# Two-layer decoder trunk on one core: the order of expert rows and front parts on each engine, from slot tables to a plan by dependences

## The chip, the core and the metric

One core of a Trainium2 chip runs the whole program; the other cores are idle. The metric is device time in microseconds (us), lower is better. Everything is float32.

## What is computed

Two layers over 512 tokens of width 1024. Each layer adds a mixer block (four head groups: chunked gating, dilated attention, short convolution, stick-breaking attention, between one input and one output projection) and then a product-key expert block (PEER). The reference, cut to what matters here:

```python
def reference(x, ...):
    for l in range(2):
        h = _rms(x, g_mix_norm[l])
        x = x + _mixer_block(h, w_in[l], ...)       # w_in 1024 x 2816, w_out 1024 x 1024
        h = _rms(x, g_ffn_norm[l])
        x = x + _peer(h, w_peer_q[l], peer_sub_keys[l], peer_u[l], peer_v[l])

def chunk(xc):                                       # 128 tokens of _peer
    q = (xc @ w_q).reshape(C, 8, 2, 128)
    s = einsum('thpd,hpkd->thpk', q, sub_keys)       # 8 heads, 2 halves, 128 keys
    sv, si = top_k(s, 16)
    cand = sv[:, :, 0, :, None] + sv[:, :, 1, None, :]
    top, pos = top_k(cand, 16)                       # 16 of 256 pairs, eidx = their experts
    g = softmax(top)
    a = einsum('thkd,td->thk', u_tab[eidx], xc)
    w = g * gelu(a)
    return einsum('thk,thkd->td', w, v_tab[eidx])
```

Every token picks 8 x 16 = 128 experts, and for each of them one row of u (4 KB) and one of v (4 KB) is read.

## The kernel before, in words

The work is cut into 8 **steps** (step s = layer s // 4, block of 128 tokens s % 4, called c). A step has 128 **expert rows** q = 128 s ... 128 s + 127: row q is one expert for each of 128 tokens, and 16 rows make a head. For each row

- GpSimd gathers 128 x 8 KB (u and v side by side, 1 MB) into one of NR = 10 places of `ring` (line 467). It waits until the indices of that head are there (`idx_ready`) and until the row that had the place ten rows earlier is used up (`v_used` or `vx_used`);
- VectorE forms the dot product with the token (u row, line 1079);
- ScalarE makes the weight and, for most rows, a 128 x 128 diagonal of it (lines 655, 661, 667);
- the v row is added: by TensorE as two 512-wide matmuls into `psY` (line 822), or by VectorE straight into x (line 1090). Here 204 rows go to VectorE, by fixed tables (`VR`, `VB`, `VF`, `BUSY_ROWS`), and 820 to TensorE.

The **front** of a step is all else: norm, input projection in 11 pieces of 1 MB of weights, attention and so on ("mixer": 4 heads of scores, bias, exponential, weighing, transpose, output; then c + 1 blocks of stick-breaking, each logits, softplus, sums, exponent, exp), output projection in 4 pieces, second norm, and per head the "top" part: query piece, key scores, top keys, top pairs, top index, gate. Steps are taken in groups (0), (1), (2, 3), (4, 5), (6, 7), which share a piece of weights. Pieces have two buffers (`wr`, NW = 2): SyncE loads the next one when the piece two before is done. Gathers of a step can only start when its top index is there, so the front of a later group runs beside the rows of an earlier one. A front part at c = 3 has four stick-breaking blocks, at c = 0 one.

What sets the order: every engine is a queue in program order, with semaphore waits inside. `part_tables` gives each front part a slot number: start of its group + rate x its place in a hand-made pattern, other rate in the top part. Each engine then walks through slots q = 0 ... 1023 and does in slot q the u row q (VectorE), the weight of row q - 1 (ScalarE), the v row q - 3 (TensorE, VectorE), and then the front parts of that slot:

```python
for q in range(SLOTS * STEPS + ROW_LAG):
    r = q - ROW_LAG
    by, m = V_NO.get(divmod(r, TOPK), (1, 0))
    if by == 0:
        ...
    for part, s, i in at_slot("pe", q):
        front(s, part, i)
```

Names the text uses: scores line 711, logits 726, sums 775 and 777, stick out 784 (the end of a mixer's chain on TensorE), gating matmul 791, pieces 694 and 698, key scores 803, transposes 680, top index 1050, first of the top keys 863.

Of the kernel before, what the change touches and what calls it, by code (L numbers as in the profile page):

```python
# [10 lines left out]
ACT = mybir.ActivationFunctionType  # L11
AX = mybir.AxisListType

P = 128
# [3 lines left out]
NC = SEQ // P  # L18
STEPS = DEPTH * NC
KD = D // P  # L20
H, HD = 4, 64
# [21 lines left out]
NG = 1  # L43
ROW_LAG = 3
VROW_LAG = 3
# [9 lines left out]
def mixer_parts(s, at):  # L55


    end = 20 + 6 * (s % NC + 1)
    p = [("act", at + t, part, 0) for t, part in
         ((14.5, "v squares"), (19, "conv taken"), (end + 2, "cat squares"), (end + 5, "catT"))]  # L60
    p += [("pe", at + t, part, 0) for t, part in ((18, "conv"), (21, "sgu"), (end, "stick out"), (end + 4, "catT"))]
    p += [("dve", at + t, part, 0) for t, part in
          ((16.5, "sgu in"), (15, "conv"), (19.5, "dil out"), (22, "sgu"), (end + 1, "stick out"), (end + 3, "cat"))]
    for h in range(H):
        o = at + 4 * h
        p += [("pe", o, "scores", h), ("dve", o + 1, "bias", h), ("act", o + 2, "dil exp", h),
              ("dve", o + 3, "weigh", h), ("pe", o + 4, "dil T", h), ("act", o + 5, "dil taken", h),
              ("pe", o + 6, "dil out", h)]
    for i in range(s % NC + 1):
        o = at + 20 + 6 * i  # L70
        p += [("pe", o, "logits", i), ("act", o + 1, "logits", i), ("dve", o + 2, "softplus", i),
              ("pe", o + 3, "sums", i), ("dve", o + 4, "exponent", i), ("act", o + 5, "stick exp", i)]
    return p, at + end


def top_parts(at):

    return [("pe", at, "key scores"), ("act", at + 0.5, "key scores"), ("dve", at + 1, "top keys"),
            ("dve", at + 2, "top pairs"), ("dve", at + 2.75, "top index"), ("act", at + 3.5, "gate exp"),
            ("dve", at + 4.5, "gate")]  # L80


def front_parts(steps):

    p, a, n = [], steps[0], len(steps)

    def add(parts, s):
        p.extend((eng, t, part, s, i) for eng, t, part, i in parts)

    for j, s in enumerate(steps):  # L90
        o = 4 * j
        add([("act", o, "norm1", 0), ("dve", o + 1, "norm1", 0), ("pe", o + 2, "hT1", 0), ("act", o + 3, "hT1", 0)], s)
    start = 4 * n
    for i in range(N_IN):
        o = start + 2 * n * i
        add([("pe", o, "piece", i), ("pe", o + n / 2, "rest of piece", i), ("act", o + 1.25 * n, "piece", i)], a)
    for j, s in enumerate(steps):
        o = start + 8 * n + 6 * j
        add([("act", o, "qk squares", 0), ("dve", o + 1, "qk", 0), ("pe", o + 3, "qk", 0), ("act", o + 4, "qk taken", 0)], s)
    out = 18 if n == 1 else 50  # L100
    for s in steps:
        parts, out = mixer_parts(s, out)
        add(parts, s)
    out += 6
    gap = 1.5 if n == 1 else 2 * n
    for i in range(N_OUT):
        o = out + gap * i
        add([("pe", o, "piece", N_IN + i), ("pe", o + n / 2, "rest of piece", N_IN + i), ("dve", o + 1.25 * n, "out", i)], a)
    second = out + N_OUT * gap - 1
    for j, s in enumerate(steps):  # L110
        o = second + 4 * j
        add([("act", o, "norm2", 0), ("dve", o + 1, "norm2", 0), ("pe", o + 2, "hT2", 0), ("act", o + 3, "hT2", 0)], s)
    top = second + 4 * n
    for h in range(PH):
        o = top + (5 * n - n // 2) * h
        add([("pe", o, "piece", N_IN + N_OUT + h), ("pe", o + n / 2, "rest of piece", N_IN + N_OUT + h),
             ("act", o + 1.25 * n, "queries", h)], a)
        for j, s in enumerate(steps):
            p.extend((eng, t, part, s, h) for eng, t, part in top_parts(o + 1.25 * n + 1 + 4 * j))
    return p, top  # L120


def part_tables():

    tables = {"act": [], "pe": [], "dve": []}
    for steps, start, rate, top_rate in GROUPS:
        parts, top = front_parts(steps)
        for eng, t, part, s, i in parts:
            tables[eng].append((start + rate * min(t, top) + top_rate * max(t - top, 0), part, s, i))
    return {eng: sorted(rows, key=lambda row: row[0]) for eng, rows in tables.items()}  # L130


PARTS = part_tables()
FIRST_SLOT = int(min(row[0] for rows in PARTS.values() for row in rows)) - 1
# [29 lines left out]
def vector_rows(J):  # L164


    return BUSY_ROWS.get(J, VR)
# [49 lines left out]
def trunk(nc, x_in, cst_in, w_in, w_out, w_q, subkeys, w_sgu, b_sgu, conv_w, g_mix, g_head, g_ffn,  # L217
# [3 lines left out]
    with ExitStack() as ctx:  # L221
# [254 lines left out]
        def _(act):  # L476
# [170 lines left out]
            for slot in range(FIRST_SLOT, 0):  # L647
                for part, s, i in at_slot("act", slot):
                    front(s, part, i)
            for q in range(SLOTS * STEPS + 1):  # L650
                if q and q % NG == 0:
                    J, k = divmod(q - NG, TOPK)
                    s, n = divmod(q - NG, SLOTS)
                    act.wait_ge(dotted, q)
                    link(nc.scalar.activation(gl[:, J % 2, k:k + NG], adot[:, J % 2, k:k + NG], ACT.Gelu_apprx_tanh))  # L655
# [4 lines left out]
                    for i in range(NG):  # L660
                        last = nc.scalar.activation(wgt[:, J % 2, k + i:k + i + 1], gate[:, s % NS, n + i:n + i + 1], ACT.Copy,  # L661
                                                    scale=gl[:, J % 2, k + i:k + i + 1])
                    last.then_inc(w_ready, 1)
                    act.wait_ge(w_ready, q // NG)
                    for i in range(NG):
                        if V_NO[J, k + i][0] == 0:
                            nc.scalar.activation(ring[:, (q - NG + i) % NR, 0:P], ident, ACT.Copy,  # L667
                                                 scale=wgt[:, J % 2, k + i:k + i + 1]).then_inc(diag_ready, 1)
                for part, s, i in at_slot("act", q):
                    front(s, part, i)  # L670
# [3 lines left out]
        def _(pe):  # L674
# [133 lines left out]
            for slot in range(FIRST_SLOT, 0):  # L808
                for part, s, i in at_slot("pe", slot):
                    front(s, part, i)  # L810
            for q in range(SLOTS * STEPS + ROW_LAG):
                r = q - ROW_LAG
                by, m = V_NO.get(divmod(r, TOPK), (1, 0))
                if by == 0:
                    s = r // SLOTS
# [9 lines left out]
                for part, s, i in at_slot("pe", q):  # L825
                    front(s, part, i)
# [3 lines left out]
        def _(dve):  # L830
# [3 lines left out]
            def link(ins):  # L834

                after(mark(ins))
# [47 lines left out]
            def front(s, part, i):  # L884
# [79 lines left out]
                elif part == "stick out":  # L964
                    dve.wait_ge(sb_out, s + 1)
                    v.tensor_copy(cat[:, 3], psO[:, :MW]).then_inc(pso_free, 1)
# [10 lines left out]
                elif part == "sgu":  # L977
                    dve.wait_ge(sgu_out, s + 1)
                    for h in range(H):
# [91 lines left out]
            for slot in range(FIRST_SLOT, 0):  # L1071
                for part, s, i in at_slot("dve", slot):
                    front(s, part, i)
            for q in range(SLOTS * STEPS + VROW_LAG + 1):
                if q < SLOTS * STEPS:
# [5 lines left out]
                r = q - VROW_LAG  # L1081
                J, k = divmod(r, TOPK)
                by, m = V_NO.get((J, k), (0, 0))
                if by:
                    xs = x[:, r // SLOTS % NC]
                    landed(dve, r)
                    dve.wait_ge(w_ready, r // NG + 1)
# [4 lines left out]
                if r >= SLOTS and r % SLOTS == 0:  # L1092
                    add_peer(r // SLOTS - 1)
                for part, s, i in at_slot("dve", q):
                    front(s, part, i)
# [40 lines left out]
```

## Time and profile before

| | us |
|---|---|
| median of 3 runs | 3071.74 (3071.59 to 3072.9) |
| the profiled execution, its own time | 3072.46 |
| its span in the trace | 3070.7 |
| TensorE busy | 2516.7 (82%) |
| VectorE busy | 2223.3 (72%) |
| ScalarE busy | 1470.0 (48%) |
| bytes moved by DMA | 1210.01 MB, of it 1073.81 MB gathers |
| mean granted TensorE clock | 0.911 |

The span is the time from the first to the last instruction; the execution's own time is 1.8 us more. Busy shares are means over stages that differ, so the text reads them stage by stage. GB/s in a stretch is what all DMA queues of the core moved in it.

### The profile page before, as it was taken

What the parts mean: (1) busy time and instruction counts of PE and PEld (TensorE: products, weight loads), DVE (VectorE), ACT (ScalarE), POOL (GpSimd) and SP (SyncE); (2) the same over time, 40 slices, a digit from 0 to 9 for tenths busy, and PEclk for the clock granted to TensorE, in tenths of its full rate; (3) what the DMA queues carried; (4) which work ended last, traced back from release to release, by engine and by line L of the source; (5) the groups of instructions that cost most, each with busy time, mean ns of one, the idle gap of its engine ahead of it and who ended that gap; (6) DMA issues with size and microseconds to landing.
All of it is one profiled execution on the core that took longest, in us unless ns stands there. A gap on an engine that the chain in (4) does not pass through costs nothing. (4 is left out here: it accounts for less than half of the span.)

```text
span 3070.7 us, 28272 instructions
## 1 busy us (share of the span) xinstructions
PE 2516.7 (82%) x7856; PEld 1431.3 (47%) x7856; DVE 2223.3 (72%) x5194; ACT 1470.0 (48%) x3968; POOL 1220.3 (40%) x1028
## 2 busy tenths in 40 slices
PE   7679778897687898997788998998889898866676
PEld 6546355563354553663354454663436444422222
DVE  2485868668769888557867888658776888866665
ACT  2154625437644555335644555437673555533333
POOL 0133434334334444434443444434444444444443
PEclk8789899998787999998998999998889999988989
DMA  6499999998789999999999999999999999999998
GB/s 277 165 403 412 421 394 421 368 407 340 295 335 409 412 397 401 421 421 421 417 421 421 417 416 412 418 420 415 378 383 410 421 421 422 413 422 422 422 422 350
DMA packets 168923, 1210.01 MB, mean 394 GB/s; under 512 B 20032, under 2 KB 20288, under 8 KB 22336
## 3 DMA queue, kind: packets, MB, share of 16 engines
q0 software_dynamic: 147456, 1073.81, 85.3%
q1 hardware_dynamic: 21312, 134.40, 10.8%
q8 instruction: 65, 1.06, 0.1%
q14 instruction: 90, 0.74, 0.1%
HBM read 1206.03 MB, written 2.10 MB: 393 GB/s over the span
## 5 line engine op out<-in xcount | busy, mean ns | idle before, releaser
L467 POOL DMA_INDIRECT ring<-in_uv,idx x1024 | 1220.1, 1192 | 1827.3 <-PE psY L822 1115.0
L822 PE MATMUL psY<-ring 128*128 128x512 f32 x3280 | 1641.6, 646 | 246.3 <-ACT ring L667 214.4
L1079 DVE CUSTOM_DVE_ANT_0 ring<-ring,htok 128x1024 f32<-128x1024 f32 x1024 | 1232.9, 1221 | 403.6 <-DMA ring<-in_uv,idx 397.0
L822 PEld LDWEIGHTS psY<-ring 128*128 128x128 f32 x3280 | 653.5, 207 | 1031.0 <-issue 1021.0
L655 ACT ACTIVATE gl<-adot 128x1 f32<-128x1 f32 x1024 | 204.1, 199 | 968.7 <-DVE adot L1079 963.8
L667 ACT ACTIVATE ring<-cst,wgt 128x128 f32<-128x128 f32 x820 | 329.3, 402 | 27.4
L694 PE MATMUL psP<-hT,wr 128*128 128x256 f32 (+1 forms) x1664 | 320.3, 349 | 1.6 <-ACT hT L504 1.0
L698 PE MATMUL psP<-wr,hT 128*128 128x256 f32 x1344 | 307.3, 383 | 16.7 <-DMA wr<-in_w_out 11.2
L661 ACT ACTIVATE wgt<-gate,gl 128x1 f32<-128x1 f32 x1024 | 301.7, 295 | 34.1
L694 PEld LDWEIGHTS psP<-hT,wr 128*128 128x128 f32 x1664 | 282.1, 198 | 71.8 <-issue 41.5
L698 PEld LDWEIGHTS psP<-wr,hT 128*128 128x128 f32 x1344 | 258.0, 193 | 86.2 <-issue 30.5
L1090 DVE SCALAR_TENSOR_TENSOR x<-ring,wgt,x 128x1024 f32<-128x1024 f32 x204 | 261.3, 1281 | 21.8 <-issue 21.8
L655 ACT ACT_TABLE_LOAD x129 | 165.5, 1283 | 2.3
L863 DVE MAX8 sv<-later 128x8 f32<-128x128 f32 x128 | 31.1, 284 | 89.9 <-ACT later L635 89.9
L775 PE MATMUL psO<-probs,cst 128*128 128x512 f32 x40 | 33.6, 934 | 71.4 <-DVE probs L945 48.5
L803 PE MATMUL psS<-probs,qdsT 128*128 128x128 f32 x256 | 44.5, 301 | 55.2 <-issue 55.2
L1079 DVE DVE_READ_ACCUMULATOR2_ANT adot<- 128x1 f32 x1024 | 84.0, 82 | 0.0
L643 ACT ACTIVATE nmax_top<-tops 128x1 f32<-128x1 f32 x64 | 12.9, 202 | 145.9 <-DVE idx L1050 145.9
L803 PEld LDWEIGHTS psS<-probs,qdsT 128*128 128x128 f32 x256 | 40.3, 207 | 89.5 <-issue 89.5
L644 ACT ACT_TABLE_LOAD x62 | 79.5, 1283 | 1.1
L680 PE MATMUL psT<-cst,hn 128*128 128x128 f32 x192 | 33.2, 330 | 54.6 <-DVE hn L1004 35.1
L1010 DVE TENSOR_TENSOR x<-x,psP 128x512 f32<-128x512 f32 (+1 forms) x20 | 11.6, 580 | 88.8 <-PE psP L698 88.8
(124 smaller groups left out, 1688.0 us busy)
## 6 DMA issues: line engine op xcount, KB each, us to landing
wr<-in_w_in SPq DMA_DIRECT2D x44, 1024.0 KB, 9.2
wr<-in_w_q SPq DMA_DIRECT2D x40, 1024.0 KB, 9.1
ring<-in_uv,idx POOLq DMA_INDIRECT x1024, 14.3
wr<-in_w_out SPq DMA_DIRECT2D x16, 1024.0 KB, 9.1
ring<-in_w_in SPq DMA_DIRECT2D x11, 1024.0 KB, 17.0
probs<-in_subkeys SPq DMA_DIRECT2D x5, 1024.0 KB, 14.4
ring<-in_w_out SPq DMA_DIRECT2D x4, 1024.0 KB, 20.2
cat<-in_g_ffn SPq DMA_DIRECT2D x5, 512.0 KB, 9.9
```

The costliest lines, as they stand in the source:

```text
L467: pool.indirect_dma_start(out=ring[:, q % NR], out_offset=None, in_=tables[s // NC], in_offset=bass.IndirectOffsetOnAxis(ap=idx[:, s % NS, ...
L644: nc.scalar.activation(gate[:, s % NS, i * TOPK:(i + 1) * TOPK], top, ACT.Exp, bias=nmax_top[:], accum_out=gsum[:]).then_inc(top_exp, 1)
L655: link(nc.scalar.activation(gl[:, J % 2, k:k + NG], adot[:, J % 2, k:k + NG], ACT.Gelu_apprx_tanh))
L661: last = nc.scalar.activation(wgt[:, J % 2, k + i:k + i + 1], gate[:, s % NS, n + i:n + i + 1], ACT.Copy, scale=gl[:, J % 2, k + i:k + i + 1])
L667: nc.scalar.activation(ring[:, (q - NG + i) % NR, 0:P], ident, ACT.Copy, scale=wgt[:, J % 2, k + i:k + i + 1]).then_inc(diag_ready, 1)
L694: last = nc.tensor.matmul(bank[:, half * n * P:(half + 1) * n * P], w[:, k, half * P:(half + 1) * P], hT[:, k, :n * P], start=(k == 0), st ...
L698: last = nc.tensor.matmul(bank[:, half * PW:(half + 1) * PW], hT[:, k, half * P:(half + 1) * P], w[:, k], start=(k == 0), stop=(k == KD - 1))
L775: last = nc.tensor.matmul(psO[:], cst[:, C_TRI:C_TRI + P], soft[:, u % 2], start=True, stop=(i == 0))
L803: last = nc.tensor.matmul(psS[:, b * P:(b + 1) * P], qT[:, QUERY_NO[a, i] % 2, b, j * P:(j + 1) * P], sub[:, 2 * i + b], start=True, stop= ...
L822: last = nc.tensor.matmul(psY[:, b * 512:(b + 1) * 512], ring[:, r % NR, 0:P], ring[:, r % NR, D + b * 512:D + (b + 1) * 512], start=first ...
L1079: v.tensor_tensor_reduce(out=u, in0=u, in1=htok[:, q // SLOTS % NS], scale=1.0, scalar=0.0, op0=ALU.mult, op1=ALU.add, accum_out=adot[:, J ...
L1090: v.scalar_tensor_tensor(out=xs, in0=ring[:, r % NR, D:], scalar=wgt[:, J % 2, k:k + 1], in1=xs, op0=ALU.mult, op1=ALU.add).then_inc(vx_us ...
```

## The change

The slot tables, the lags and the tables of VectorE rows are gone. A planner (`plan_orders`) plays the program through on the host with a cost for each part, dependences (`needs`), counts of shared buffers and a model of loads and gathers, and writes down in which order each engine begins its rows and parts. An engine that is free takes, of what can begin, the item with the earliest due time. A front part is due by the old pattern (`front_times`, other starts and rates), a u row at its landing - 2 us, the weight of a row at the end of its u row + 3.5, a v row at its landing + 6. A v row goes to VectorE only where three or more wait for TensorE, none for VectorE, and the next u row has not landed: 61 rows in all, 963 to TensorE. Instructions, bytes, buffers and gathers are as before, apart from three things: 143 more rows are TensorE's (186 go to it, 43 to VectorE), each with a diagonal made on ScalarE, and VectorE has a wait for `cat_squared` ahead of "sgu" and "stick out".

```diff
-NG = 1
-ROW_LAG = 3
-VROW_LAG = 3
-GROUPS = [((0,), -72, 1.00, 1.00), ((1,), 22, 1.00, 1.10), ((2, 3), 129, 0.70, 1.30), ((4, 5), 339, 1.15, 1.30), ((6, 7), 597, 0.97, 1.55)]
+GROUPS = [((0,), -72, 1.00, 1.00), ((1,), -22, 0.85, 0.95), ((2, 3), 120, 0.85, 1.35), ((4, 5), 355, 1.50, 1.45), ((6, 7), 606, 1.10, 1.40)]
+SLOT_US = 2.65
+U_SLACK = -2.0
+R_SLACK = 3.5
+V_SLACK = 6.0
+PE_ROWS = 3
+MARGIN = 0.2
...
+def plan_orders():
...
+            due[eng, part, s, i] = 150 + SLOT_US * (start + rate * min(t, top) + top_rate * max(t - top, 0))
...
+    def choices(eng):
+        c = []
+        for (e, part), keys in classes.items():
...
+            key = keys[0]
+            if missing[key] or ready[key] > now + 1e-9:
+                continue
+            if (eng, part) in HELD and not left[HELD[eng, part]]:
+                continue
...
+            c.append((due[key], key))
+        if eng == "dve":
+            if state["u"] < SLOTS * STEPS and state["u"] in landed:
+                c.append((landed[state["u"]] + U_SLACK, ("u", state["u"])))
...
+        if eng in rows and rows[eng]:
+            q = rows[eng][0]
+            if ("r", q) in done and (eng == "dve" or q // SLOTS <= state["x"]):
+                c.append((landed[q] + V_SLACK, ("v", q)))
+        return c
+
+    def begin(eng, key):
...
+        elif key[0] == "r":
+            state["r"] += 1
+            by[key[1]] = int(len(rows["pe"]) >= PE_ROWS and len(rows["dve"]) == 0 and state["u"] not in landed)
+            rows["dve" if by[key[1]] else "pe"].append(key[1])
...
+                if c:
+                    begin(eng, min(c)[1])
...
+ORDERS, ROW_BY = plan_orders()
...
-VR = (3, 7, 11, 15)
-VB = (1, 3, 5, 7, 9, 11, 13, 15)
-VF = ()
-BUSY_ROWS = {J: VB for J in range(9, 16)}
-BUSY_ROWS.update({J: VF for lo, hi in ((6, 8), (16, 21), (31, 37), (47, 54)) for J in range(lo, hi)})
...
-            for q in range(SLOTS * STEPS + ROW_LAG):
-                r = q - ROW_LAG
-                by, m = V_NO.get(divmod(r, TOPK), (1, 0))
-                if by == 0:
-                    s = r // SLOTS
+            for name, *where in ORDERS["pe"]:
+                if name == "v":
+                    r = where[0]
+                    m, s = V_NO[divmod(r, TOPK)][1], r // SLOTS
...
-                for part, s, i in at_slot("pe", q):
+                else:
+                    part, s, i = where
                     front(s, part, i)
...
                 elif part == "stick out":
                     dve.wait_ge(sb_out, s + 1)
+                    if s:
+                        dve.wait_ge(cat_squared, s)
```

**First place: TensorE, the first stick-breaking blocks of step 3.** `psS<-qdsT,ksT` is the logits of a block, `psO<-probs,cst` and `psO<-later,cst` its sums, `psO<-tms,sgw` the gating, and `psY<-ring x2` one expert row. Before:

```order
L726 MATMUL psS<-qdsT,ksT 128x128 x4
L822 MATMUL psY<-ring 128x512 x2
L791 MATMUL psO<-tms,sgw 128x64 x4
L775 MATMUL psO<-probs,cst 128x512
L822 MATMUL psY<-ring 128x512 x2
L726 MATMUL psS<-qdsT,ksT 128x128 x4
L822 MATMUL psY<-ring 128x512 x2
L775 MATMUL psO<-probs,cst 128x512
L777 MATMUL psO<-later,cst 128x512
L822 MATMUL psY<-ring 128x512 x4
```

The same place in the change:

```order
L1025 MATMUL psS<-qdsT,ksT 128x128 x4
L1117 MATMUL psY<-ring 128x512 x2
L1090 MATMUL psO<-tms,sgw 128x64 x4
L1117 MATMUL psY<-ring 128x512 x4
L1025 MATMUL psS<-qdsT,ksT 128x128 x4
L1074 MATMUL psO<-probs,cst 128x512
L1117 MATMUL psY<-ring 128x512 x4
L1025 MATMUL psS<-qdsT,ksT 128x128 x4
L1074 MATMUL psO<-probs,cst 128x512
L1076 MATMUL psO<-later,cst 128x512
L1117 MATMUL psY<-ring 128x512 x12
L1025 MATMUL psS<-qdsT,ksT 128x128 x4
```

The logits of the next block now stand ahead of the sums of this one, and all rows between are TensorE's. Counted over the whole order, from the first scores to stick out of a step (in row numbers q, on TensorE): step 1 takes 32 rows before and 15 in the change, step 2 takes 26 and 31, step 3 takes 32 and 40, step 4 takes 29 and 18, step 5 takes 38 and 30, step 6 takes 36 and 37, step 7 takes 44 and 49. Steps 2 and 3 together take 58 and 71, of which VectorE has 29 and 8.

**Second place: TensorE, the top part of step 1.** `psP<-hT,wr x16` is a query piece, `psS<-probs,qdsT x2` the key scores of a head. Before, from the query piece of head 2:

```order
L694 MATMUL psP<-hT,wr 128x128 x16
L822 MATMUL psY<-ring 128x512 x4
L803 MATMUL psS<-probs,qdsT 128x128 x2
L822 MATMUL psY<-ring 128x512 x6
L694 MATMUL psP<-hT,wr 128x128 x8
L822 MATMUL psY<-ring 128x512 x2
L694 MATMUL psP<-hT,wr 128x128 x8
L822 MATMUL psY<-ring 128x512 x2
L803 MATMUL psS<-probs,qdsT 128x128 x2
```

In the change, from the query piece of head 4:

```order
L993 MATMUL psP<-hT,wr 128x128 x16
L1117 MATMUL psY<-ring 128x512 x2
L1102 MATMUL psS<-probs,qdsT 128x128 x2
L1117 MATMUL psY<-ring 128x512 x2
L993 MATMUL psP<-hT,wr 128x128 x16
L1102 MATMUL psS<-probs,qdsT 128x128 x2
L993 MATMUL psP<-hT,wr 128x128 x16
L1102 MATMUL psS<-probs,qdsT 128x128 x2
L993 MATMUL psP<-hT,wr 128x128 x16
L979 MATMUL psT<-cst,hn 128x128 x8
L1102 MATMUL psS<-probs,qdsT 128x128 x2
L1117 MATMUL psY<-ring 128x512 x20
```

Before, every piece has rows within and behind it; in the change the last heads' pieces follow each other and ten rows come in one run behind them. On VectorE it is the same place: between the u rows 100 and 101 stand top pairs and top index of head 3 and the whole top parts of heads 4 to 7, where before three to four u rows stand in each head's.

## Rows read from the trace of the kernel before

**Rows 1.** The page: span, bytes moved.

```profile
span 3070.7 us, 28272 instructions
...
DMA packets 168923, 1210.01 MB, mean 394 GB/s; under 512 B 20032, under 2 KB 20288, under 8 KB 22336
```

**Rows 2.** Windows: us, busy PE, PEld, DVE, ACT, POOL (x count), clock, DMA share, GB/s.

```profile
0.00:128.00 128.00, 88.16 (x436) 75.11 (x436) 37.18 (x136) 29.16 (x61) 0.20 (x4) 0.84 0.50 193
...
150.00:500.00 350.00, 284.02 (x1064) 173.01 (x1064) 260.81 (x656) 172.56 (x463) 128.82 (x109) 0.89 1.00 409
...
550.00:700.00 150.00, 137.91 (x515) 96.99 (x516) 94.82 (x180) 59.15 (x168) 47.19 (x42) 0.93 0.95 379
700.00:900.00 200.00, 136.65 (x409) 72.93 (x408) 153.84 (x283) 134.04 (x263) 68.84 (x57) 0.80 0.83 314
900.00:1250.00 350.00, 298.82 (x904) 170.78 (x903) 297.71 (x830) 172.48 (x496) 151.12 (x124) 0.93 1.00 407
...
1400.00:1650.00 250.00, 198.26 (x569) 105.12 (x569) 187.56 (x366) 135.47 (x351) 109.57 (x92) 0.90 1.01 420
...
2165.00:2350.00 185.00, 160.91 (x508) 89.67 (x507) 131.14 (x239) 112.42 (x262) 76.73 (x66) 0.90 0.95 382
...
2700.00:3050.00 350.00, 232.47 (x418) 87.76 (x416) 214.60 (x316) 114.05 (x393) 163.39 (x139) 0.87 1.01 422
```

**Rows 3.** Waits of all engines in 700:900: us in total, times, longest.

```profile
POOL ring L467 <- DVE x L1090: 77.6, 23, 10.1
POOL ring L467 <- PE psY L822: 47.8, 14, 8.0
...
PE psO L775 <- DVE probs L945: 25.4, 5, 6.5
```

**Rows 4.** TensorE's timeline, steps 2 and 3: start, us, line (first scores, stick out).

```profile
678.63 0.91 PE L711 MATMUL psS<-kdT,qdsT 64*128 64x384 f32 x2
...
757.99 2.89 PE L784 MATMUL psO<-vs,tmq 128*128 128x64 f32 x24
760.81 1.12 PE L711 MATMUL psS<-kdT,qdsT 64*128 64x512 f32 x2
...
870.08 3.79 PE L784 MATMUL psO<-vs,tmq 128*128 128x64 f32 x32 [0.36 <-ACT tmq L600]
```

**Rows 5.** TensorE's timeline: step 0's scores and stick out; scores of steps 4, 5; step 7.

```profile
44.86 0.48 PE L711 MATMUL psS<-kdT,qdsT 64*128 64x128 f32 x2
...
78.16 1.97 PE L784 MATMUL psO<-vs,tmq 128*128 128x64 f32 x8 [2.63 <-ACT tmq L600]
...
1379.86 0.48 PE L711 MATMUL psS<-kdT,qdsT 64*128 64x128 f32 x2
...
1455.27 0.70 PE L711 MATMUL psS<-kdT,qdsT 64*128 64x256 f32 x2
...
2167.90 1.12 PE L711 MATMUL psS<-kdT,qdsT 64*128 64x512 f32 x2
...
2286.01 3.68 PE L784 MATMUL psO<-vs,tmq 128*128 128x64 f32 x32
```

**Rows 6.** TensorE's timeline: a piece that waited, three rows, half a piece of two steps.

```profile
410.96 5.73 PE L698 MATMUL psP<-wr,hT 128*128 128x256 f32 x16 [10.72 <-DMA wr<-in_w_out]
416.53 5.31 PE L822 MATMUL psY<-ring 128*128 128x512 f32 x12
...
894.50 3.62 PE L698 MATMUL psP<-wr,hT 128*128 128x256 f32 x16
```

**Rows 7.** The page's group of the u rows.

```profile
L1079 DVE CUSTOM_DVE_ANT_0 ring<-ring,htok 128x1024 f32<-128x1024 f32 x1024 | 1232.9, 1221 | 403.6 <-DMA ring<-in_uv,idx 397.0
```

**Rows 8.** VectorE's timeline: top keys' first, top index of step 0, head 0.

```profile
121.50 0.49 DVE L863 MAX8 sv<-later 128x8 f32<-128x128 f32 x2 [10.09 <-ACT later L635]
...
129.13 0.17 DVE L1050 SCALAR_TENSOR_TENSOR idx<-pick 128x16 int32<-128x16 f32 x1
```

**Rows 9.** Tile ring on POOL: a gather's time from issue to landing.

```profile
DMA to landing us min/median/max: 5.5/14.3/22.9
```

More of the change, by code:

```diff
@@ L76, in top_parts, with front_times @@
[L76 to L83, printed above, removed]
+SLOT_US = 2.65
[4 more added lines that the diff above has]
+MARGIN = 0.2
+def front_times(steps):
     p, a, n = [], steps[0], len(steps)
-    def add(parts, s):
-        p.extend((eng, t, part, s, i) for eng, t, part, i in parts)
@@ L120, in front_parts @@
     return p, top
-def part_tables():
-    tables = {"act": [], "pe": [], "dve": []}
-    for steps, start, rate, top_rate in GROUPS:
[L127 to L134, printed above, removed]
@@ L137, in at_slot, with cost @@
-def at_slot(eng, slot):
-    return [row[1:] for row in PARTS[eng] if slot <= row[0] < slot + 1]
+def cost(eng, part, s, i):
+    n, w = len(GROUP_OF[s]), s % NC + 1
+    if part in ("piece", "rest of piece"):
+        if eng == "act":
+            return 0.3 * n
+        whole = CB <= i < N_IN or i >= N_IN + N_OUT
+        return 3.5 * n / 2 if whole or n == 2 else 3.5 if part == "piece" else 0.0
+    return {"pe": {"hT1": 1.1, "qk": 1.1, "catT": 1.1, "hT2": 1.1, "scores": 0.25 * w, "dil T": 0.15 * w, "dil out": 0.15 * w,
+                   "conv": 0.3, "sgu": 0.5, "logits": 1.2, "sums": 0.9 if i == 0 else 1.75, "stick out": 0.5 * w,
+                   "key scores": 0.5},
+            "act": {"norm1": 1.2, "norm2": 1.2, "hT1": 2.4, "catT": 2.4, "hT2": 1.1, "qk squares": 1.1, "qk taken": 1.3,
+                    "v squares": 0.4, "dil exp": 0.3 + 0.1 * w, "dil taken": 0.2 + 0.1 * w, "logits": 2.4, "stick exp": 0.7,
+                    "conv taken": 0.4, "cat squares": 1.1, "queries": 0.6, "key scores": 0.4, "gate exp": 0.6},
+            "dve": {"norm1": 2.9, "qk": 5.0, "bias": 0.3 + 0.3 * w, "weigh": 0.2 + 0.15 * w, "dil out": 0.6, "softplus": 1.3,
+                    "exponent": 1.2, "stick out": 0.4, "sgu in": 3.2, "sgu": 0.7, "conv": 2.6, "cat": 4.6, "out": 0.35 * n,
+                    "norm2": 3.6, "top keys": 3.0, "top pairs": 2.8, "top index": 2.9, "gate": 0.2}}[eng][part]
@@ L142, in numbers @@
+ORDERS, ROW_BY = plan_orders()
 def numbers(eng, *names):
-    rows = [row[1:] for row in PARTS[eng] if row[1] in names]
+    rows = [key[1:] for key in ORDERS[eng] if key[0] == eng and key[1] in names]
     return {row: n for n, row in enumerate(rows)}
@@ L1070, in _ @@
             dve.wait_ge(s_cst, 16)
[L1071 to L1075, printed above, removed]
+            for name, *where in ORDERS["dve"]:
+                if name == "u":
+                    q = where[0]
                     J, k = divmod(q, TOPK)
@@ L1091, in _ @@
                                            op0=ALU.mult, op1=ALU.add).then_inc(vx_used, 1)
[L1092 to L1094 removed]
+                elif where[0] == "x":
+                    add_peer(where[1])
+                else:
+                    part, s, i = where
                     front(s, part, i)
```

399 lines of the change are left out of this document (335 added, 64 removed).

## The prediction, made before the changed kernel was run

> **What bounds the kernel now.** Read in this order: the bytes, the windows by stage, the waits where a stage is slow, then the timeline there. The core moves 1210 MB in a span of 3070.7 us [rows 1]. In the last long stretch, 2700 to 3050, nothing but rows is left and the queues move 422 GB/s, the most of any stretch, while TensorE is busy 232 of 350 us [rows 2]. So 422 GB/s is what this mix of transfers gets, and 1210 MB at that rate is 2867 us. The other 203 us are stretches in which the queues were not full. The loss of a stretch is its length x (1 - GB/s / 422), from [rows 2]:
>
> - 0 to 128, before the first gather: 69
> - 150 to 500, rows of step 0 beside the front of step 1: 11
> - 550 to 700, input projection of steps 2 and 3: 15
> - 700 to 900, their mixers: 51
> - 900 to 1250, their top parts: 12
> - 1400 to 1650, mixers of steps 4 and 5: 1
> - 2165 to 2350, mainly the mixer of step 7: 18
>
> The rest (26) is the first gathers, the end, and small change. An order of instructions moves no bytes; it can only win or lose in this list, and outside of the first 128 us and the end some 120 us are to be had at most.
>
> Why 700 to 900 is slow: GpSimd waits there for ring places, 77.6 us for VectorE's v rows and 47.8 for TensorE's [rows 3], while TensorE is busy only 137 of 200 us and VectorE 154 [rows 2]. No engine is full; rows stand in program order behind front parts that wait for each other, as the sums for softplus, 25.4 us [rows 3]. The mixer of step 2 takes from 678.6 to 760.9 (82 us) and that of step 3 from 760.8 to 873.9 (113 us) [rows 4]. Its chain of parts sets this, not the rows: a row needs 1 MB / 422 GB/s = 2.49 us, and the 26 and 32 rows in it need 65 and 80. The excess, 17 + 33 = 50, is the measured loss of 51. That agreement is what I build on: **a mixer costs the queues what its chain needs beyond the rows laid into it.**
>
> **The change, term by term** (against the profiled execution, 3072.46 us).
>
> Mixers of steps 2 and 3. They now have 31 and 40 rows, 77 and 100 us of transfers. With the old chains of 82 and 113 the loss is 5 + 13 = 18 instead of 50: **-32**. The logits of the next block now run ahead of the sums of this one, so that VectorE's and ScalarE's work on them lies beside the sums; a block of step 3 cost about 15 us of its 113. Steps 2 and 3 have seven blocks; I take a little over 1 us from each: **-8**; at most the remaining 18, at least 0.
>
> Mixer of step 7. 2167.9 to 2289.7 is 122 us [rows 5], for 44 rows, 110 us. The order gives it 49 rows, 122 us; step 6 keeps its 36 to 37. Of the 18 lost, **-13**.
>
> Mixers of steps 4 and 5. They lose nothing now: step 4 takes 75.4 us [rows 5] for 29 rows (72). The change gives them 18 and 30 rows, 45 and 75 us. What their chains need is not shown, since transfers pace them. Bounds for step 4: step 0's mixer, the same c with no rows in it, took 44.9 to 80.1, 35 us [rows 5], and above 75. I take 50, and for step 5 no more than its 75: **+6**. Ends 0 and +48 (30 in step 4, 18 in step 5, whose mixer takes 93 of its 95 us from transfers). Step 1, squeezed from 32 rows to 15, has seven weight pieces among them, so 55 us of transfers; its chain is longer than step 0's 35 us by one block of some 15, and has rows in it: I give it +5, and take back 3 for the piece of w_out that TensorE waited 10.7 us for [rows 6], whose rows now stand otherwise: **+2**, ends -8 and +25.
>
> Top part of step 1. VectorE does the tops of heads 3 to 7 with no u row between. One head is 121.5 to 129.3, 7.8 us [rows 8]; a u row is 1.22 + 0.08 [rows 7]. From u row 90 to 110 that is 8 x 7.8 + 20 x 1.3 = 88 us, against 20 gathers and 10 weight pieces at 2.49, 75 us. The excess of 13 is partly covered by what is queued: a gather lands 14.3 us after its issue where 5.5 is the least [rows 9], so some 9 us of transfers are in store. **+6**, ends 0 and +20 (weight pieces that queue behind gathers, as the 10.7 us).
>
> Projection of steps 2 and 3. Half a piece is 3.62 us, a row on TensorE 5.31 / 3 = 1.77 (a row is four records) [rows 6]. Before, rows 130 to 160: 11 x 7.2 + 18 x 1.77 + transposes 2 = 113 us against 41 transfers, 102; an excess of 11, with 15 lost. In the change, rows 112 to 138 with 13 of them VectorE's: 79 + 13 x 1.77 + 2 = 104 against 92. The same within 2: **-2**, ends -10 and +10.
>
> More rows on TensorE. 143 x 1.77 = 253 us of work, and VectorE loses as many rows of 1.3. In 2700 to 3050 TensorE has 118 us idle [rows 2] for 32 of them (57 us). The other 111 (197 us) go where 380 of 2550 us are idle, most of it in mixers. I cost them at **0**; the cover is gone if that idle time is waiting that stays, which is the slow rival below.
>
> Before the first gather. In step 0 "sgu in" now stands before the weighing of head 0 and "conv" before that of head 2; by the old durations head 3 leaves VectorE some 3 us later, and half a query piece stands ahead of the first key scores: **+4**, ends -4 and +8. The end: the last row goes over diagonal and TensorE, **+1**. The two new waits on `cat_squared` ask for work of the step before and cost 0. Top parts of the later groups have the same work: 0.
>
> Sum: -32 - 8 - 13 + 6 + 2 + 6 - 2 + 0 + 4 + 1 = -36. 3072.5 - 36 = 3036, and as the median is 0.7 below the profiled execution, **3036** holds for it too.
>
> TensorE's clock belongs here. In 700 to 900 it was granted 0.80 on average, so some 40% of that time ran at 1.2 instead of 2.4 GHz, with 63 of 200 us idle; in 900 to 1250, with 51 of 350 idle, it was 0.93 [rows 2]. The sum takes each duration as the trace has it and counts nothing for the clock. The Trainium skill (TensorE: Matmul & The Clock Gate, HAM oscillation) says that gaps in TensorE's work put it to half clock and an unbroken supply keeps it at full; the two windows agree. By that rule alone the rows moved to TensorE would partly pay for themselves and the time would come out below the sum, as in the first rival.
>
> **Rivals.**
>
> *Faster: rows flow in all mixers.* If blocks overlap and TensorE, fuller, is rarely at half clock, the losses of 700 to 900, 2165 to 2350 and 550 to 700 go: -51 - 18 - 15 = -84, and the start and the block cost 8: 2996. For it: no engine is full there. Against: chains through three engines remain, and 10 ring places.
>
> *No difference.* A mixer's chain stretches with what is laid into it: 113 us for step 3 with 32 rows, 122 for step 7 with 44 [rows 4, 5]. If it does so at 13 us for 8 rows, and the squeezed steps 1, 4 and 5 lose 20, the gain is gone: 3072. This is also the case in which the plan's costs are so far from the chip's that its order waits as the old one did.
>
> *Slower: TensorE becomes the bound.* Place: the mixers and the pieces beside them. If its idle time in 700 to 900 (63 us) stays and 21 rows come to it (37 us) beside 137 of work, the stage takes 237 instead of the 160 forecast, +77. In the mixers of 4 and 5, 52 us idle and 13 rows more: +23; in 6 and 7 the like, +30. It decides once more than about a quarter of that idle time is left (130 / 4 = 33, the gain). With half of it left: 3036 + 65 = 3101. For it: 186 rows leave VectorE in all, and rows at half clock cost twice. Against: planned orders put rows where old ones put waits, and VectorE gets free.
>
> **How the numbers follow.** Forecast (3010 to 3060) 0.52, rows flow 0.17, no difference 0.12, TensorE the bound 0.19. A difference under 0.2% (6 us) is what a measurement of this kernel can't tell from none. Faster gets the first two and a little of the third, 0.71; same 0.10; slower 0.19. The likeliest case's own range is 3010 to 3060. The range for 8 in 10 goes from 2988, just under the fast rival, to 3098, which leaves out the worse half of the slow one.
>
> **What would show it.** Right: 700 to 900 (step 2's and 3's mixers) at 380 GB/s or more instead of 314; GpSimd's waits for VectorE's rows nearly gone and its waits for TensorE's larger; the granted clock above 0.911; step 3's mixer in 100 to 115 us; a dip of GB/s near 400 to 500 where step 1's top parts stand together; first gather at 130 to 138 us instead of 129.6. Wrong: TensorE near 100% busy in the mixers with queues under 400 GB/s (the slow rival), mixers of steps 4 and 5 under 390 GB/s (their chains need more than I took), or a first gather much later.

## The result, and the profile after

The changed kernel takes 3031.11 us (median of 4 runs, 3028.67 to 3033.62) beside 3071.66 us before (3067.65 to 3072.9): ratio 0.9874, 95% interval 0.9861 to 0.9886. It is 40.6 us faster; the forecast was 36. Every median here and below leaves out the executions in the chip's slow state, of which there were two (E1 once, 3777.73 us; the kernel before once, 6970.06 us). The page of its profile:

```profile
span 3029.1 us, 29251 instructions
...
PE 2654.6 (88%) x8428; PEld 1473.6 (49%) x8428; DVE 2062.3 (68%) x5051; ACT 1513.4 (50%) x4098; POOL 1163.1 (38%) x1028
...
DMA packets 168926, 1210.08 MB, mean 399 GB/s; under 512 B 20032, under 2 KB 20288, under 8 KB 22336
...
L1117 PE MATMUL psY<-ring 128*128 128x512 f32 x3852 | 1815.5, 615 | 274.1 <-ACT ring L965 269.4
```

The bytes are those of [rows 1]. The granted clock is 0.961 on average (0.911 before). So the 41.6 us between the spans must lie in stretches where the queues are not full. Windows of the changed kernel, with columns as in [rows 2]:

```profile
0.00:128.00 128.00, 92.26 (x476) 79.42 (x477) 39.72 (x148) 31.15 (x66) 0.20 (x4) 0.84 0.50 195
150.00:400.00 250.00, 223.56 (x801) 128.39 (x800) 170.14 (x428) 132.55 (x352) 89.81 (x81) 0.98 1.01 421
...
450.00:550.00 100.00, 77.59 (x342) 55.41 (x343) 80.26 (x244) 39.00 (x124) 23.22 (x19) 0.86 0.72 291
550.00:633.00 83.00, 80.60 (x337) 62.23 (x337) 57.17 (x114) 25.88 (x79) 28.14 (x25) 1.00 1.00 400
633.00:821.00 188.00, 169.00 (x518) 83.15 (x517) 131.79 (x248) 150.97 (x313) 85.06 (x71) 0.94 0.97 394
821.00:1150.00 329.00, 298.86 (x925) 171.10 (x925) 278.85 (x798) 165.55 (x474) 136.37 (x120) 0.97 1.01 421
1150.00:1200.00 50.00, 34.89 (x102) 18.98 (x101) 31.82 (x65) 22.42 (x74) 17.87 (x15) 0.82 0.91 365
...
1400.00:1500.00 100.00, 94.41 (x280) 47.68 (x279) 71.03 (x144) 76.86 (x183) 44.99 (x39) 0.95 1.00 410
...
1900.00:2050.00 150.00, 140.54 (x510) 92.48 (x509) 105.81 (x214) 74.19 (x185) 52.28 (x46) 0.95 1.00 410
2050.00:2212.00 162.00, 150.78 (x449) 73.64 (x448) 100.30 (x185) 130.29 (x280) 74.61 (x64) 0.97 0.99 395
```

By the loss formula of the prediction, stretch by stage (us of queue time lost):

| stage | before | after | difference | forecast |
|---|---|---|---|---|
| before the first gather | 69.5 | 68.9 | -0.6 | +4 |
| rows of step 0, front of step 1 up to its last tops | 10.8 | 0.7 | -10.1 | +2 |
| last tops of step 1 (before 500:550, after 450:550) | 0.1 | 31.0 | +30.9 | +6 |
| projection and mixers of steps 2, 3 (550:900; 550:821) | 66.5 | 16.8 | -49.7 | -42 |
| their top parts, up to 1150 (before 1250) | 12.4 | 0.8 | -11.6 | 0 |
| projection of step 4, first part (1150:1200) | in the row above | 6.8 | +6.8 | not seen |
| mixers of steps 4, 5 | 1.2 | 2.8 | +1.6 | +6 |
| 1500 (before 1650) to 2350, with the mixers of 6, 7 | 23.6 | 16.6 | -7.0 | -13 |
| all other stretches (first gathers, last rows, end) | 19.3 | 18.1 | -1.2 | +1 |
| sum | 203.4 | 162.5 | -40.9 | -36 |

The sum is 0.7 us from the 41.6 between the spans, as the rates are whole numbers. The total is near, but three stages are far off: one lost 25 us more than forecast, and two came out 12 us better each. What stands behind GpSimd now, for the whole run (us in total, times, longest):

```profile
POOL ring L769 <- PE psY L1117: 1597.5, 773, 38.5
POOL ring L769 <- DVE idx L1350: 157.0, 6, 129.0
...
POOL ring L769 <- DVE x L1388: 2.0, 1, 2.0
```

Before, VectorE's rows held it for 426.9 us and TensorE's for 1115.0. A wait with full queues costs nothing (ten places are always in use); the one of 38.5 us does. TensorE's timeline of steps 2 and 3, to be laid beside [rows 4]:

```profile
633.63 0.91 PE L1010 MATMUL psS<-kdT,qdsT 64*128 64x384 f32 x2
...
714.99 1.12 PE L1010 MATMUL psS<-kdT,qdsT 64*128 64x512 f32 x2
...
817.71 3.68 PE L1083 MATMUL psO<-vs,tmq 128*128 128x64 f32 x32
```

Both mixers take 633.6 to 821.4, 188 us with 71 rows, where 195 us had 58.

### The profile page after: what moved, and what is told of

Read it like the earlier page. It is cut to its first block and busy times, and to the rows that moved or that the text cites. A ratio compares the mean times of both kernels' runs of the same rounds, so it can differ in the third digit from the quotient of the medians.

```text
span 3029.1 us, 29251 instructions
## 1 busy us (share of the span) xinstructions
PE 2654.6 (88%) x8428; PEld 1473.6 (49%) x8428; DVE 2062.3 (68%) x5051; ACT 1513.4 (50%) x4098; POOL 1163.1 (38%) x1028
## 3 DMA queue, kind: packets, MB, share of 16 engines
q1 hardware_dynamic: 21312, 134.40, 10.9%
## 5 line engine op out<-in xcount | busy, mean ns | idle before, releaser
L1117 PE MATMUL psY<-ring 128*128 128x512 f32 x3852 | 1815.5, 615 | 274.1 <-ACT ring L965 269.4
L769 POOL DMA_INDIRECT ring<-in_uv,idx x1024 | 1162.9, 1136 | 1838.0 <-PE psY L1117 1597.5
L1117 PEld LDWEIGHTS psY<-ring 128*128 128x128 f32 x3852 | 723.0, 195 | 1221.1 <-issue 1214.0
L965 ACT ACTIVATE ring<-cst,wgt 128x128 f32<-128x128 f32 x963 | 386.7, 402 | 31.4
L993 PEld LDWEIGHTS psP<-hT,wr 128*128 128x128 f32 x1664 | 275.3, 195 | 51.0 <-issue 19.1
L1388 DVE SCALAR_TENSOR_TENSOR x<-ring,wgt,x 128x1024 f32<-128x1024 f32 x61 | 78.3, 1283 | 34.2 <-issue 34.2
L997 PE MATMUL psP<-ring,hT 128*128 128x256 f32 x192 | 46.7, 408 | 2.9 <-ACT hT L810 2.9
L1347 DVE TENSOR_TENSOR fm<-pos,cst 128x512 f32<-128x512 uint32 x64 | 44.3, 692 | 2.2
L1348 DVE TENSOR_TENSOR fm<-fm,si 128x512 f32<-128x512 f32 x64 | 44.3, 692 | 2.2
L1349 DVE TENSOR_REDUCE pick<-fm 128x32 f32<-128x512 f32 x64 | 43.9, 686 | 2.2
```

What stands on the lines that cost most here:

```text
L769: pool.indirect_dma_start(out=ring[:, q % NR], out_offset=None, in_=tables[s // NC], in_offset=bass.IndirectOffsetOnAxis(ap=idx[:, s % NS, ...
L965: nc.scalar.activation(ring[:, q % NR, 0:P], ident, ACT.Copy, scale=wgt[:, J % 2, one_col]).then_inc(diag_ready, 1)
L993: last = nc.tensor.matmul(bank[:, half * n * P:(half + 1) * n * P], w[:, k, half * P:(half + 1) * P], hT[:, k, :n * P], start=(k == 0), st ...
L997: last = nc.tensor.matmul(bank[:, half * PW:(half + 1) * PW], hT[:, k, half * P:(half + 1) * P], w[:, k], start=(k == 0), stop=(k == KD - 1))
L1117: last = nc.tensor.matmul(psY[:, b * 512:(b + 1) * 512], ring[:, r % NR, 0:P], ring[:, r % NR, D + b * 512:D + (b + 1) * 512], start=first ...
L1347: link(v.tensor_tensor(hot, pos[:, 1:3].unsqueeze(3).broadcast_to(shape), iota, ALU.is_equal))
```

## The experiments

Twelve kernels, each timed beside the kernel before (its medians were 3069.0 to 3071.9). A ratio is to the kernel before, with its 95% interval behind it. The theory: the gain lies in the mixers of steps 2 and 3, and the loss of 31 us at 450 to 550 in the run of tops on VectorE.

### Is it the order or the choice of rows?

**E1: the old slots, but with the 61 rows of the plan on VectorE.**

```diff
 def vector_rows(J):
-    return BUSY_ROWS.get(J, VR)
+    return tuple(q % TOPK for q in TO_VECTOR if q // TOPK == J)
```

> The old slot tables and lags, but the 61 VectorE rows of the plan in place of the old 204. Order theory (the gain is the rows laid into the mixers of steps 2, 3 and 7): those mixers keep 26, 32 and 44 rows, so their loss stays, 700 to 900 remains near 314 GB/s, and only VectorE's relief in the top parts shows: 3055 to 3075. Rows theory (the gain is VectorE rid of 143 v rows that stood in its queue): most of the 41 us come, 3030 to 3045, and 700 to 900 rises to 380 GB/s.

**E2: the plan, but with the old 204 rows on VectorE.**

```diff
-            by[key[1]] = int(len(rows["pe"]) >= PE_ROWS and len(rows["dve"]) == 0 and state["u"] not in landed)
+            by[key[1]] = int(key[1] % TOPK in BUSY_ROWS.get(key[1] // TOPK, VR))
```

> The plan, with VectorE's rows fixed to the old tables (204). The plan shifts with it: 26, 38 and 43 rows in the mixers of steps 2, 3, 7, and VectorE's run of top parts without a u row at step 1 is longer. Order theory: mixers lose (82 - 65) + (113 - 95) = 35 instead of 16, the run at step 1 some 5 more: 3050 to 3062. Rows theory: back to the time before, 3065 to 3080, with GpSimd waiting for VectorE's rows in every mixer.

Measured: E1 3080.6 us, ratio 1.0028 (1.0011 to 1.0045); E2 3077.31 us, ratio 1.0025 (1.0014 to 1.0035). **Each half alone is no faster than before (0.3% slower); only together do they give 41 us.** E1 lies above both of its ranges. E2 lies in the range of the rows theory (3065 to 3080), and GpSimd does wait for VectorE's rows in the mixers of 2 and 3 (53 us in 652 to 822, 73 us in 679 to 874 before), but little is lost there: the time goes elsewhere. The 61 rows of E1 were picked for the times of the plan; whether another choice would help the old slots was not tested. GpSimd's waits, first in E1, then in E2:

```profile
POOL ring L469 <- PE psY L824: 1532.7, 795, 15.5
...
POOL ring L469 <- DVE x L1092: 110.8, 32, 9.4
```

```profile
POOL ring L776 <- PE psY L1124: 1330.9, 602, 36.7
POOL ring L776 <- DVE x L1395: 241.1, 71, 8.7
```

In E1 the waits for VectorE's rows are down to 110.8 us, and the mixers of 2 and 3 still lose 54 of 200 us: the waits have only gone over to TensorE. So [rows 3], read as "VectorE's rows hold the ring", named who came last and not the cause. In E2 the mixers are largely cured: they take 171 us for 64 rows and lose 18, where the kernel before lost 46. But 65 us are lost between 450 and 700 and 15 between 1000 and 1100, where VectorE has the tops to do; that it can't carry the rows there as well is the likely reason, not a separate finding. First scores of step 2 and stick out of step 3 on TensorE, in E1, then in E2:

```profile
684.30 0.91 PE L713 MATMUL psS<-kdT,qdsT 64*128 64x384 f32 x2
...
873.21 3.68 PE L786 MATMUL psO<-vs,tmq 128*128 128x64 f32 x32
```

```profile
651.85 0.91 PE L1017 MATMUL psS<-kdT,qdsT 64*128 64x384 f32 x2
...
818.76 3.68 PE L1090 MATMUL psO<-vs,tmq 128*128 128x64 f32 x32
```

### What shortened the mixers?

**E7: narrower mixers for steps 2 and 3 in the plan.**

```diff
-((2, 3), 120, 0.85, 1.35)
+((2, 3), 120, 0.70, 1.35)
```

> The change with rate 0.70 instead of 0.85 for the front of steps 2 and 3: their mixers get 24 and 27 rows instead of 31 and 40, nearly the old 26 and 32, under the planned order. Rows-laid theory: the chains take the 85 and 106 us that they take in the change, rows need 60 and 67, so the stretch from the first scores of step 2 to stick out of step 3 loses 25 + 39 = 64 us instead of 16: 3070 to 3080, less what later stretches give back (some of the 48 come back only if a later stage loses now, and none does): 3065 at least. Rival (the plan's order itself shortens the chains, and rows laid matter little): chains shrink to 70 and 80 us, a loss of 10 + 13 = 23, and 3031 to 3042.

**E8: the logits of a block no longer ahead of the sums of the one before.**

```diff
+        if i:
+            d += [("act", "stick exp", s, i - 1)]
```

> The change, with the logits of a stick-breaking block allowed only behind the last exp of the block before. The plan then lays 34 and 43 rows into the mixers of steps 2 and 3 (31 and 40), and 40 and 52 in steps 6 and 7. If running ahead shortens a chain by about 1 us per block (my term of 8): chains of 2 and 3 take 88 and 110 us or more, about what the added rows cover, 3031 to 3041. Rival, it shortens them by far more (3 us per block, 20 in steps 2 and 3 and as much in 6 and 7): 3050 or more. Rival, by nothing: 3031 or faster.

**E13: both edits.**

> The plan with the rate of group (2, 3) at 0.70, and the logits of a block no longer ahead of the sums of the one before. Steps 2 and 3 have 30 and 32 rows. If the logits ahead are what shortened their mixers, the two take 185 to 195 us together (195 with 58 rows under the slots). If it is the planned order as a whole, they take 165 to 172 (171 with 64 rows and the old 204 rows on VectorE) and the time is 3035 to 3060.

Measured: E7 3067.46 us, ratio 0.9991 (0.9982 to 1.0001); E8 3035.54, ratio 0.9886 (0.9869 to 0.9903); E13 3075.82, ratio 1.0016 (1.0006 to 1.0026). The same two instructions in E7, then in E13:

```profile
629.67 0.91 PE L1010 MATMUL psS<-kdT,qdsT 64*128 64x384 f32 x2
...
786.03 3.68 PE L1083 MATMUL psO<-vs,tmq 128*128 128x64 f32 x32
```

```profile
621.93 0.91 PE L1012 MATMUL psS<-kdT,qdsT 64*128 64x384 f32 x2
...
785.93 3.68 PE L1085 MATMUL psO<-vs,tmq 128*128 128x64 f32 x32
```

Both mixers together, in the kernels that bear on this, with a row at 2.49 us:

| kernel | order | rows in them | they take | beyond the rows |
|---|---|---|---|---|
| before | slots | 58 | 195 | 51 |
| E1 | slots | 58 | 193 | 48 |
| E7 | plan | 51 | 160 | 33 |
| E13 | plan, logits not ahead | 62 | 168 | 13 |
| E2 | plan, old 204 rows | 64 | 171 | 11 |
| after | plan | 71 | 188 | 11 |
| E8 | plan, logits not ahead | 77 | 204 | 12 |

From 62 to 77 rows the time follows the rows (36 us for 15, 2.4 each), so the chain isn't what is seen there. With 51 rows it takes 160. The kinds of order separate: under the slots 48 to 51 us go beyond the rows with either choice of VectorE's rows, under the plan 11 with either (E2 and the changed kernel). **Of the 195 us that the prediction took for the chain, at least 24 were waits that the slot order put in (E2 has the same VectorE rows and six rows more), and 35 if the seven rows that E7 leaves out cost the chain nothing.** The logits ahead aren't what removes them: E13 takes 168 us without them, not the 185 to 195 that would have shown it, and E8 as a whole can't be told from the changed kernel (0.9886 and 0.9874, with intervals that overlap). Nor is it the clock: in its mixers E1 was granted 0.90 and still takes 48 us beyond the rows, E2 0.86 with 11; and E7 and E13, at 0.962 and 0.964 over the whole run, are no faster than the kernel before. Which detail of the planned order does it, and how far below 160 the chain alone is, was not separated. What E7 shows for the prediction: with 20 rows fewer in the two mixers the whole gain is gone (0.9991), so the plan wins only together with the wider mixers. It agrees with the law on rows in its total only (3065 at least was expected): 600 to 850 loses 47 us where the changed kernel loses 16, and 850 to 1000 another 16. E13 came out slower than its 3035 to 3060, since 450 to 600 (40 us lost) and 700 to 1050 (38) suffer too; the last was not followed up.

### The run of tops in step 1

VectorE's u rows in the changed kernel, around the run:

```profile
456.77 1.22 DVE L1377 CUSTOM_DVE_ANT_0 ring<-ring,htok 128x1024 f32<-128x1024 f32 x1
457.91 0.08 DVE L1377 DVE_READ_ACCUMULATOR2_ANT adot<- 128x1 f32 x1
499.70 1.22 DVE L1377 CUSTOM_DVE_ANT_0 ring<-ring,htok 128x1024 f32<-128x1024 f32 x1
```

TensorE and GpSimd there:

```profile
502.87 18.99 PE L1117 MATMUL psY<-ring 128*128 128x512 f32 x40 [14.79 <-ACT ring L965]
```

```profile
506.69 1.98 POOL L769 DMA_INDIRECT ring<-in_uv,idx  x1 [38.46 <-PE psY L1117]
...
546.60 0.94 POOL L769 DMA_INDIRECT ring<-in_uv,idx  x1 [18.82 <-PE psY L1117]
```

No u row runs for 42 us. The ring fills and GpSimd stands for 38.5 us; then ten rows come at once, and the run of projection pieces behind them makes the second stop of 18.8.

**E3: step 1 starts later, as before the change.**

```diff
-((1,), -22, 0.85, 0.95)
+((1,), 22, 1.00, 1.10)
```

> The change with the start and rates of step 1 as before (22, 1.00, 1.10). The top parts of heads 3 to 7 of step 1 are then spread, with u rows between; its mixer gets 29 rows instead of 15. If the run of top parts costs the queues 31 us in 450 to 550 (277 and 305 GB/s there), 25 to 31 of them come back: 3000 to 3008. Rival: VectorE must do the tops anyway and step 1 is bound by it wherever they stand, or the loss moves to the projection of steps 2 and 3, which starts 15 rows later: 3020 to 3031.

Measured: 3028.85 us, ratio 0.9867 (0.985 to 0.9883). The rival was right: 450 to 500 loses 3 instead of 17, and 500 to 550 loses 9 instead of 14, but the loss goes to the projection of steps 2 and 3, with TensorE full (550 to 850 loses 28 instead of 17):

```profile
550.00:600.00 50.00, 49.03 (x192) 35.43 (x191) 33.57 (x62) 18.00 (x56) 16.93 (x14) 1.00 0.95 349
```

**E12: VectorE's parts are due no earlier than 10 us before they can begin, so that u rows come between them; with E4's hold, below.**

```diff
-            c.append((due[key], key))
+            c.append((max(due[key], ready[key] - 10.0) if eng == "dve" else due[key], key))
```

> The variant with hT1 of step 4 held, in which a front part on VectorE counts as due no earlier than 10 us before it could begin, so that no part that is late by a hundred us keeps every u row out. No run of top parts without a u row is left. If that run is what costs 31 us in 450 to 550: that stretch loses 10 or less, the projection behind it up to 15 as in the kernel before, and the time is 3002 to 3012. Rival, the loss only moves on into the projection of steps 2 and 3, as it did when step 1 began later: 3018 to 3026.

Measured: 3021.86 us, ratio 0.9848 (0.9832 to 0.9865), 1 us from E4 without the cap. Yet the run is gone: 450 to 550 loses 5 us instead of 31. It comes back elsewhere, and not where the rival had it: GpSimd waits for the first indices of steps 4 and 6, which are now ready no rows ahead of their gathers (seven and five ahead in the changed kernel), and 1600 and 2300 lose 13 and 10 us:

```profile
1628.57 0.94 POOL L770 DMA_INDIRECT ring<-in_uv,idx  x1 [23.12 <-DVE idx L1351]
...
2346.40 0.94 POOL L770 DMA_INDIRECT ring<-in_uv,idx  x1 [22.40 <-DVE idx L1351]
```

**E10: E3, E4's hold, and every other row from 112 to 147 (the projection) on VectorE.**

```diff
+                               or 112 <= key[1] < 148 and key[1] % 2)
```

> The variant with step 1 later, with hT1 of step 4 held until u row 340, and with every odd row of 112 to 147 sent to VectorE whatever waits. The later step 1 left 33 us of loss in 500 to 750, with TensorE busy 49 of 50 us in 550 to 600 and VectorE 34. If TensorE is the bound there, eight more rows of 1.77 us off it give back 8 to 14 us, and the hold gives 5: 3008 to 3016. Rival, the loss is the chain of the projection (pieces, two buffers, copies) and not TensorE's load: 3022 to 3026.

Measured: 3013.16 us, ratio 0.9821 (0.9805 to 0.9837), as expected. 550 to 850 loses 12 us, where E3 lost 28: the projection was bound by TensorE, and VectorE had room. But 1600 and 2300 lose 7 and 9 for late first indices (19.5 and 17.4 us of GpSimd's wait).

### The dip at 1150 that nobody forecast

ScalarE in the changed kernel:

```profile
1167.59 2.17 ACT L810 ACTIVATE hT<-psT,gain_t 128x128 f32<-128x128 f32 x8 [9.84 <-DMA g_col<-in_g_qk]
```

hT1 (ScalarE's copy of a step's transposed, normed input, with its gains) wants layer 2's parameters for step 4. SyncE issues them only after the last index of step 3. The plan knows that index but not the load behind it, so it puts hT1 too early, with eleven rows' weights behind it. GpSimd stands for 18.3 us.

**E4: hT1 of step 4 not before u row 340.**

```diff
-                d += [("dve", "top index", before[-1], PH - 1)]
+                d += [("dve", "top index", before[-1], PH - 1), ("u", HOLD)]
```

> The change with hT1 of step 4 held back until u row 340, so that ScalarE does not stand 10 us at the parameters of layer 2 with ten rows behind it. Theory: the dip in 1150 to 1200 (365 GB/s, 6.8 us) goes, 3024 us, plus or minus 4 for the shifted row counts behind it (mixers of steps 4 to 7 get 16, 29, 33 and 51 rows). Rival: another wait takes its place in the same stretch and nothing is won: 3031.

Measured: 3022.83 us, ratio 0.9852 (0.9835 to 0.9868), as expected. The wait is gone, and 1150 to 1200 moves 411 GB/s instead of 365:

```profile
1150.00:1200.00 50.00, 38.55 (x114) 21.23 (x113) 30.86 (x61) 24.16 (x78) 17.14 (x16) 0.93 1.01 411
```

So a wait of 9.8 us on an engine that is 50% busy cost 5.5 us in that stretch, by what stood behind it; the total fell by 8, of which the rest is within the spread of the runs.

### Everything together

**E14: E10, groups (4, 5) and (6, 7) ten rows earlier (starts 345 and 596). E15: E12 with E10's rows and the same starts.**

> The run with rows 112 to 147 shared out, hT1 of step 4 held and a later start of step 1, and now the starts of groups (4, 5) and (6, 7) ten rows earlier. If the dips at 1600 and 2300 (7 and 9 us there) come from a first top index that is ready only one or two rows before its gathers, GpSimd's waits for the indices go but for the first, and the time is 2996 to 3003. If the dips are TensorE's, they move with the mixers and the time stays over 3010.

> VectorE's parts due no earlier than 10 us before they can begin, hT1 of step 4 held, rows 112 to 147 shared out, starts of (4, 5) and (6, 7) ten rows earlier. The run at 450 to 550 stays small (5 us) and the dips at 1600 and 2300 (13 and 10) go if they were the late first top index: 2994 to 3004. If step 1's mixer with 15 rows and the projection of 2 and 3 keep their losses, 3005 to 3015.

Measured: E14 3010.66 us, ratio 0.9796 (0.978 to 0.9813); **E15 2996.26 us, ratio 0.9754 (0.9737 to 0.977), the best of all, and 35 us under the changed kernel.** In both the waits for indices at 1600 and 2300 are gone. In E14 the dip at 1150 is back (9.2 us), since the earlier start brings hT1 ahead of the parameters again; without it the time would be near 3002 (an estimate), within the 2996 to 3003 that it missed. E15:

```profile
450.00:550.00 100.00, 86.18 (x373) 59.00 (x374) 94.37 (x272) 55.06 (x158) 37.11 (x30) 0.91 0.97 393
633.00:821.00 188.00, 175.74 (x568) 89.29 (x567) 143.05 (x269) 149.59 (x334) 91.22 (x74) 0.98 1.01 421
1150.00:1200.00 50.00, 35.14 (x125) 24.11 (x126) 24.67 (x46) 18.42 (x62) 11.54 (x10) 0.83 0.90 344
1600.00:1650.00 50.00, 50.00 (x165) 30.22 (x164) 43.16 (x123) 27.18 (x75) 21.84 (x19) 1.00 1.01 421
```

Its mixers of 2 and 3 take 173 us for 69 rows (172 us of transfers): they lose 1 us. Against the changed kernel it wins 24 us at 450 to 550 and 13 at 550 to 850.

**E17: E15 with the hold at row 350.**

```diff
-HOLD = 340
+HOLD = 350
```

> The run of 2996 us with hT1 of step 4 held until u row 350 instead of 340, five rows (12 us) later. There ScalarE waits 9.9 us for layer 2's parameters at 1149 to 1159 and 1150 to 1200 loses 9.2 us. If the row number of the hold is what was wrong once everything ran earlier, the wait and the dip go (under 2 us) and the time is 2986 to 2991. If the hold only moves the stop into the projection of step 4, the loss comes back between 1200 and 1350 and the time stays at 2994 to 3000.

Measured: 2998.35 us, ratio 0.9769 (0.9753 to 0.9785); not told apart from E15. The wait for the parameters is gone and 1150 to 1200 loses 1.8 instead of 9.2, but 1200 to 1250 loses 4.3 that it did not before. The rest doesn't come from the edit: up to row 345 both orders are the same, and still 600 to 850 loses 5 us here and 0.5 in E15. One profile of a stretch is that uncertain.

## Why the prediction was right, and where its steps failed

It was right on the sign, the total (3031 for 3036) and the place of the main gain. That the total came within 5 us is in part luck: the loss in step 1's tops was 25 us more than forecast, step 4's projection cost 7 unforeseen, and two stages that came out 12 us better each, with 8 more won in steps 2 and 3, made up for them. "What would show it" held for 700 to 900 (394 GB/s in the mixers, 380 asked), the waits for VectorE's rows (2.0 us), the clock (0.961) and step 3's mixer (715.0 to 821.4, 106 us; 100 to 115 asked). Term by term:

- **Mixers of steps 2 and 3 (-32 and -8):** with their projection -50 for -42. The size was right, the reason only in part. "With the old chains of 82 and 113" fails: the planned order needs 171 us at most for both with the old VectorE rows (E2) and 160 with seven rows fewer (E7), so rows laid in were not the whole lever. By the same count, the old 58 rows in a chain of 160 would lose some 16 instead of 51 (an estimate; not run). The overlap of logits and sums, to which -8 was given, is not the cause (E8, E13).
- **Rows on TensorE (0):** right for the whole, wrong as a separate item. Under the slots they cost: by its ratio E1 is 9 us over the kernel before (3 to 14). Without them the plan is 46 us worse (E2). The two parts of the change have no prices of their own.
- **Top part of step 1 (+6, ends 0 and +20):** measured +31, outside my ends. I set work against transfers over u rows 90 to 110, as if the surplus could be spread. In the trace it stands in one piece: 42 us without a u row, near the five heads at 7.8 us that the prediction itself had. The 9 us "in store" were there: GpSimd stops at 468, and until 480 the queues still move 409 GB/s. But then all ten places are full, and from 480 to 507 they move 52. The first stop (38.5 us, 6.2 MB moved in it) loses 24 us, the second (18.8 us, 6.5 MB) 3, and the time between them another 3.
- **150 to 500 (+2) and the later top parts (0):** measured -10 and -12. Before, both lost 11 to 12 us in small pieces; the plan loses 1 in each. "The same work: 0" forgot that the losses there were the order's too.
- **Step 4's projection:** +7, not seen. I took the new dependence list as complete, and counted SyncE's weight pieces but not its parameters, which land 10.9 us after their issue.
- **Before the first gather (+4):** -0.6; the first gather is issued at 129.4 us, not 130 to 138. That "head 3 leaves VectorE 3 us later" didn't reach the first key scores, which start at 120.3.
- **Mixers of 4, 5 (+6) and 7 (-13):** +2 and -7 for the whole stretch, with signs as forecast, a third and a half of the size.

Of the rivals, the slow one (TensorE the bound) exists, but small: TensorE is busy 80.6 of 83 us in the projection of 2 and 3, where 4 us are lost. In the mixers, where I had placed it, it has 19 us idle of 188. The fast rival's 2996 is what E15 reaches, with four more edits, so the number is a coincidence. The clock, counted at nothing, rose: the rows' matmuls in the mixers take 622 ns each instead of 721, at a granted clock of 0.94 for 0.79. What that gave back was not separated; E7 and E13 had the higher clock too and were no faster than the kernel before.

## What to carry to other kernels

Where many queues feed one ring, average work against average transfers hides the loss: look for the longest stretch in which the ring's first consumer does nothing for it, and charge all of it that goes beyond what is already issued (12 us here). A chain's length read from a trace holds the waits of the order it ran in; only a version with fewer rows in it shows how short it can be. And an order that is planned on the host is as good as its list of dependences: a small load that it doesn't know (9.8 us here), or a first index with no rows to spare (23 us), undoes what the plan wins elsewhere.

## What the runs showed of the hardware

The queues move 421 to 423 GB/s, over 50 us or more, in every stretch that isn't starved, in all kernels, with gathers and weight pieces mixed, with TensorE busy 66% (2700 to 3050 of the kernel before) or all the time (1600 to 1650 of E15). The Trainium skill (HBM Reference, Specifications) gives a core some 358 GB/s as its share, and around 425 when it streams alone; the second agrees with this case, where the other cores are idle.

I had not expected the clock to follow so closely. The mixers of 2 and 3 ran at a granted clock of 0.79 with TensorE busy 68% of the time, and at 0.94 with 90%; in the dips at 450 and 1150 it fell to 0.86 and 0.82. The kernel before in its mixers:

```profile
678.00:874.00 196.00, 133.42 (x385) 66.83 (x384) 152.96 (x280) 141.30 (x264) 68.25 (x58) 0.79 0.85 323
```

A parameter load of 2 KB, the third of seven issued one behind the other beside gathers, took 11 us to be usable: in E15 it is issued at 1148.2 and hT1 starts at 1159.2.

```profile
1148.19 0.43 SPq L715 DMA_DIRECT2D g_col<-in_g_qk  x1
```

```profile
1159.15 2.17 ACT L812 ACTIVATE hT<-psT,gain_t 128x128 f32<-128x128 f32 x8 [9.88 <-DMA g_col<-in_g_qk]
```
